# Latent heads: value products on half the columns, side by side, with the row sums made elsewhere

## The reference

```
def attend(q, k, v, scale):              # one head; context queries see the 256 context keys,
    s = q @ k.T * scale                  # latent queries all 768 keys
    p = exp(s - rowmax(s))
    return (p @ v) / rowsum(p)           # v is 64 wide
y  = attend(...) * silu(z)               # per head, then all heads beside each other
x  = x + gate * (concat(y_gla, y_latent, y_gqa) @ w_out)
```

## Time and profile before

| | |
|---|---|
| median of 3 runs | 957.71 us (954.34 to 958.46) |
| profiled execution, its own time | 957.99 us |
| its span in the trace | 956.2 us |
| TensorE busy | 911.3 us, 95% of the span |
| VectorE, ScalarE, GpSimd busy | 508.1, 432.6, 160.6 us |
| latent heads of layer 0 in the trace | 266.4 to 393.9 us |
| latent heads of layer 1 in the trace | 730.9 to 830.6 us |

### The profile page before, as it was taken

How to read it: one execution, slowest core, us unless ns; L and a number is a source line. 1 busy time by engine, 2 the same in 40 slices (tenths; PEclk the granted TensorE clock), 3 DMA queues, 4 the chain that set the end, 5 groups by cost and what they waited for, 6 DMA issues and landing times.

```text
span 956.2 us, 12848 instructions
## 1 busy us (share of the span) xinstructions
PE 911.3 (95%) x4607; PEld 665.2 (70%) x4607; DVE 508.1 (53%) x893; ACT 432.6 (45%) x809; POOL 160.6 (17%) x193
## 2 busy tenths in 40 slices
PE   4799999999999999899999999999999999899995
PEld 3488889888666666555588887889775656445584
DVE  4455424533547676756534655553646767455524
ACT  5434434321334545666831745543324445556712
POOL 1020000001442223002162000000026311002150
PEclk9899999999999999999999999999999999999998
DMA  9740230320202222222027102321401000222022
GB/s 342 276 125 22 50 83 22 89 66 2 88 1 88 89 88 88 89 91 86 1 77 215 65 22 67 92 64 42 113 23 67 1 1 1 89 88 89 1 110 89
DMA packets 67869, 74.21 MB, mean 78 GB/s; under 512 B 6148, under 2 KB 47456, under 8 KB 67680
## 3 DMA queue, kind: packets, MB, share of 16 engines
q1 hardware_dynamic: 61392, 60.24, 19.9%
q0 software_dynamic: 4016, 12.77, 3.8%
q10 hardware_dynamic: 2400, 0.38, 0.2%
HBM read 69.18 MB, written 4.19 MB: 77 GB/s over the span
## 4 chain that ended last, share of the span: by engine, by line
PE 85%; DVE 6%; ACT 4%; issue 3%; POOL 1%; ACTq 1%; DVEq 0%; POOLq 0%
PE pv L1868 12%; PE bank L1640 10%; PE bank L1641 9%; PE bank L1642 9%; PE bank L1954 4%; PE bank L1956 4%; PE bank L1955 4%; PE bank L1829 4%; PE bank L1795 2%; PE bank L1921 2%; PE bank L1915 2%; PE bank L1687 2%; PE bank L1686 2%; PE bank L1688 2%; PE bank L1591 2%
## 5 line engine op out<-in xcount | busy, mean ns | idle before, releaser
L1640 PE MATMUL bank<-hA_parts,W_parts 128*128 128x512 f32 (+1 forms) x480 | 174.6, 364 | 5.1 <-DVE h_low_parts L1155 5.1
L1641 PE MATMUL bank<-hA_parts,W_parts 128*128 128x512 f32 (+1 forms) x496 | 174.5, 352 | 0.0
L1004 ACT ACTIVATE hA<-bank 128x512 f32<-128x512 f32 (+1 forms) x168 | 93.3, 562 | 89.6 <-PE bank L1917 65.3
L1454 DVE TENSOR_REDUCE mxp<-bank 128x1 f32<-128x384 f32 x192 | 96.0, 551 | 33.7 <-PE bank L1829 33.2
L1640 PEld LDWEIGHTS bank<-hA_parts,W_parts 128*128 128x128 f32 x480 | 92.4, 192 | 22.4 <-issue 10.8
L1642 PE MATMUL bank<-h_low_parts,W_parts 128*128 128x512 f32 (+1 forms) x300 | 106.0, 353 | 0.0
L1641 PEld LDWEIGHTS bank<-hA_parts,W_parts 128*128 128x128 f32 x496 | 95.4, 192 | 13.2 <-issue 1.9
L1868 PE MATMUL pv<-hA,vg 128*128 128x512 f32 (+1 forms) x168 | 81.8, 571 | 4.4 <-ACT hA L1004 4.3
L1163 DVE TENSOR_TENSOR W_parts<-W,W_parts 128x1024 fp32r<-128x1024 f32 x43 | 52.5, 1222 | 36.7 <-ACT W_parts L711 36.7
L1868 PE MATMUL pv<-hA,h_low 128*128 128x512 f32 (+1 forms) x144 | 69.3, 562 | 0.0
L711 ACT ACTIVATE W_parts<-W 128x1024 fp32r<-128x1024 f32 x43 | 45.3, 1057 | 41.2 <-DMA W<-in_w_in 40.7
(11 more groups left out here) (291 smaller groups left out, 1914.3 us busy)
## 6 DMA issues: line engine op xcount, KB each, us to landing
W<-in_w_in SPq DMA_DIRECT2D x39, 512.0 KB, 4.1
W<-in_w_mod SPq DMA_DIRECT2D x8, 2048.0 KB, 8.1
W<-in_w_out SPq DMA_DIRECT2D x4, 2048.0 KB, 8.0
gqk<-in_w_mod SPq DMA_DIRECT2D x2, 1536.0 KB, 9.9
cqkv<-in_w_mod SPq DMA_DIRECT2D x2, 1536.0 KB, 14.2
XA<-in_x SPq DMA_DIRECT2D x4, 512.0 KB, 7.4
XA<-in_x POOLq DMA_DIRECT2D x4, 512.0 KB, 6.8
x_between_layers<-XA POOLq DMA_DIRECT2D x4, 512.0 KB, 3.0
```

The lines of the kernel that those rows point to most:

```text
L1004: act.activation(prob[slot % 4][:, 0:nq], ps("sc", l, h, q0, kt)[:, 0:nq], ACT.Exp, scale=MLA_SCALE if h < MLA_H else GQA_SCALE)\
L1454: dve.tensor_reduce(mxp[:, t, half:half + 1], ps("mx", l, h, q0, t, half)[:, 0:384], AX, ALU.max).then_inc(*up("part_max", l, h, q0, t, half))
L1640: pe.matmul(p[:, 0:c[1]], high[:, k, :], h_hi[:, k, toks], start=(k == 0), stop=False)
L1641: pe.matmul(p[:, 0:c[1]], low[:, k, :], h_hi[:, k, toks], start=False, stop=False)
```

## The change

For the latent heads alone:

- `vm` holds the values alone, [128, 6, 64] for each key tile. `pv` makes two products for each unit, one for each half of the queries, with the same 64 columns of values as weights; they write partitions 0 to 63 and 64 to 127 of one bank. Context and latent queries of a head share a bank now.
- The products are held back: `flush(2, most)` does nothing until 6 units are pending (layer 0) or 5 (layer 1), then it multiplies all but two; the rest follows ahead of `max_rows` of the next head. So a head has two runs of value products.
- The row sums: GpSimd adds probability buffers in pairs (`add_pair`: one of 256 columns for the context, two of 512, and one more add of the two), VectorE adds the last pair (`last_pair`), and TensorE multiplies the results by ones (`den`, three pairs of half-width products in layer 0, two in layer 1), after `project_k` of the next head.
- `recip` becomes one Ln and one Exp on all 128 partitions for both kinds of queries (`latent_recip`). `normalise` becomes two half-width products and the gate (`latent_normalise`), and that of the context queries moves from inside `maxima` to the start of the next head, ahead of that of the latent queries.
- GpSimd's `k_pad` and `q_pad(0)` move into head 5, behind that head's first `add_pair` in layer 0 and behind the sums of head 4 in layer 1. The ones in `vm` are no longer written.
- Six buffers `prob` in place of four.

```diff
+PROBS = 6
...
-        vm = [e.rearrange("p (r c) -> p r c", r=3) for e in
-              [low[:, T + 576 * t:T + 576 * t + 576] for t in range(TILES - 1)] +
-              [tz[:].rearrange("p a b -> p (a b)")[:, 0:576]]]
+        vm = [low[:, T + 384 * t:T + 384 * t + 384].rearrange("p (h v) -> p h v", h=MLA_H) for t in range(TILES)]
+        pair_sum = {0: [low[:, 4 * T + 512:5 * T]], 256: [low[:, 4 * T:4 * T + 512], XA[:, 7 * T - 256:7 * T + 256]]}
+        prob += [tz[:, i, :] for i in range(2)]
...
+        def half_cols(q0, nq):
+            c = 0 if q0 else 256
+            return slice(c, c + nq // 2)
...
-                for h in heads[1:MLA_H]:
-                    if h < len(out_tiles(l)):
-                        gla_in(out_tiles(l)[h])
-                        pool.wait_ge(*at("Sbd", l, out_tiles(l)[h], 1))
-                        two_diagonals(out_tiles(l)[h])
-                        pool.wait_ge(*at("A_both", l, out_tiles(l)[h]))
-                pool.wait_ge(*at("filled", "qp", l, MLA_H - 1, LAT))
-                for g in range(2):
-                    if g:
-                        pool.wait_ge(*at("k_pad", l, 0, 1))
-                    pool.memset(k_low[g][64:96, :].bitcast(F32), 0.0).then_inc(*up("k_pad", l, g, 0))
-                    pool.memset(k_low[g][96:97, :].bitcast(F32), 1.0).then_inc(*up("k_pad", l, g, 1))
-                pool.wait_ge(*at("k_pad", l, 1, 1))
-                for b in range(2):
+                def add_pair(h, q0, nq, i):
+                    slot, to = slot_of(l, h, q0) + 2 * i, min(i, 1)
+                    pool.wait_ge(*at("prob", l, slot + 1))
+                    if h:
+                        pool.wait_ge(*at("filled", "den", l, h - 1))
+                    if i:
+                        pool.wait_ge(*at("kd_exp", l, 1))
+                    pool.tensor_tensor(pair_sum[q0][to], prob[slot % PROBS][:, 0:nq],
+                                       prob[(slot + 1) % PROBS][:, 0:nq], ALU.add).then_inc(*up("pair_sum", l, h, q0, i))
+                def query_pad(b):
                     pool.wait_ge(*at("filled", "sc", l, MLA_H + b - 2, 256, TILES - 1))
                     pool.memset(q_high[b][64:96, :].bitcast(F32), 0.0).then_inc(*up("q_pad", l, b))
-                pool.wait_ge(*at("q_pad", l, 1))
+                    pool.wait_ge(*at("q_pad", l, b))
+                for h in heads[:MLA_H]:
+                    tile = out_tiles(l)[h + 1] if h + 1 < len(out_tiles(l)) else None
+                    if tile is not None:
+                        gla_in(tile)
+                    if len(qbs(l)) == 2:
+                        add_pair(h, *qbs(l)[0][:2], 0)
+                    if tile is not None:
+                        pool.wait_ge(*at("Sbd", l, tile, 1))
+                        two_diagonals(tile)
+                        pool.wait_ge(*at("A_both", l, tile))
+                    if h == MLA_H - 1:
+                        pool.wait_ge(*at("filled", "qp", l, MLA_H - 1, LAT))
+                        pool.wait_ge(*(at("pair_sum", l, h, 0, 0) if len(qbs(l)) == 2 else at("both_sums", l, h - 1)))
+                        for g in range(2):
+                            pool.memset(k_low[g][64:96, :].bitcast(F32), 0.0).then_inc(*up("k_pad", l, g, 0))
+                            pool.wait_ge(*at("k_pad", l, g, 0))
+                            pool.memset(k_low[g][96:97, :].bitcast(F32), 1.0).then_inc(*up("k_pad", l, g, 1))
+                            pool.wait_ge(*at("k_pad", l, g, 1))
+                        query_pad(0)
+                    for i in range(2):
+                        add_pair(h, *qbs(l)[-1][:2], i)
+                    pool.wait_ge(*at("pair_sum", l, h, 256, 1))
+                    pool.tensor_tensor(pair_sum[256][0], pair_sum[256][0], pair_sum[256][1], ALU.add)\
+                        .then_inc(*up("both_sums", l, h))
+                pool.wait_ge(*at("both_sums", l, MLA_H - 1))
+                query_pad(1)
...
+                def latent_recip(h):
+                    n = sum(nq // 2 for _, nq, _ in qbs(l))
+                    act.wait_ge(*at("filled", "den", l, h))
+                    if recips:
+                        act.wait_ge(*at("o_scaled", *recips[-1]))
+                    act.activation(rd[:, 0:n], ps("den", l, h)[:, 0:n], ACT.Ln).then_inc(*up("den_ln", l, h))
+                    let_go(("den", l, h), "den_ln", l, h)
+                    act.wait_ge(*at("den_ln", l, h))
+                    act.activation(rd[:, 0:n], rd[:, 0:n], ACT.Exp, scale=-1.0).then_inc(*up("recip", l, h))
+                    recips.append((l, h, 256))
...
+                def latent_normalise(h, q0, nq):
+                    cols, r, n2 = half_cols(q0, nq), 64 * (h % 2), nq // 2
+                    dve.wait_ge(*at("pv_filled", l, h, 256))
+                    if last_y[0]:
+                        dve.wait_ge(*at("y_attn", *last_y[0]))
+                    dve.wait_ge(*at("recip", l, h))
+                    for e in range(2):
+                        half = slice(64 * e, 64 * e + 64)
+                        dve.scalar_tensor_tensor(out=un[r:r + 64, n2 * e:n2 * e + n2], in0=pv_banks[h % 2][half, cols],
+                                                 scalar=0.5, in1=rd[half, cols], op0=ALU.mult, op1=ALU.mult)\
+                            .then_inc(*up("o_scaled", l, h, q0))
+                    dve.wait_ge(*at("o_scaled", l, h, q0))
+                    y = Y[r:r + 64, 2 + h // 2, q0:q0 + nq]
+                    dve.tensor_tensor(y, un[r:r + 64, 0:nq], y, ALU.mult).then_inc(*up("y_attn", l, h, q0))
+                    last_y[0] = (l, h, q0)
+                def last_pair(h):
+                    slot = slot_of(l, h, 256) + 4
+                    dve.wait_ge(*at("both_sums", l, h))
+                    dve.wait_ge(*at("prob", l, slot + 1))
+                    dve.tensor_tensor(pair_sum[256][1], prob[slot % PROBS], prob[(slot + 1) % PROBS], ALU.add)\
+                        .then_inc(*up("last_sum", l, h))
...
-                        normalise(h - 1, *qbs(l)[-1][:2])
+                        for q0, nq, nk in qbs(l) if h - 1 < MLA_H else qbs(l)[-1:]:
+                            normalise(h - 1, q0, nq)
...
+                    if h < MLA_H:
+                        last_pair(h)
...
+                        o, n2 = pv_banks[h % 2][:, half_cols(q0, nq)], nq // 2
+                        for e in range(2):
+                            mm = pe.matmul(o[64 * e:64 * e + 64], vm[kt][:, h, :], prob[sl % PROBS][:, n2 * e:n2 * e + n2],
+                                           start=(kt == 0), stop=(kt == nkt - 1), skip_group_check=True)
                     else:
-                        v = vg[:, kt, (h - MLA_H) // 3, 64 * e:64 * e + P]
-                    if h == 0 and kt == 0:
-                        pe.wait_ge(*at("vm", l, TILES - 1, 1))
-                        pe.wait_ge(*at("vg", l, TILES - 1, 1))
-                    mm = pe.matmul(pv_banks[i % 2][:, 0:nq], v, prob[sl % 4][:, 0:nq], start=(kt == 0),
-                                   stop=(kt == nkt - 1))
-                    if kt == nkt - 1:
+                        v = vg[:, kt, (h - MLA_H) // 3, 64 * (h % 2):64 * (h % 2) + P]
...
+                def den(h):
+                    p = open_("den", l, h)
+                    for q0, nq, nk in qbs(l):
+                        cols, n2 = half_cols(q0, nq), nq // 2
+                        parts = [(pair_sum[q0][0], ("both_sums", l, h)), (pair_sum[q0][1], ("last_sum", l, h))]\
+                            if q0 else [(pair_sum[q0][0], ("pair_sum", l, h, q0, 0))]
+                        for i, (part, ready) in enumerate(parts):
+                            pe.wait_ge(*at(*ready))
+                            for e in range(2):
+                                mm = pe.matmul(p[64 * e:64 * e + 64, cols], ones[:, 0:64], part[:, n2 * e:n2 * e + n2],
+                                               start=(i == 0), stop=(i == len(parts) - 1), skip_group_check=True)
+                    close(mm, "den", l, h)
+                def flush(keep_n, most=1):
+                    if len(pend) >= most:
+                        while len(pend) > keep_n:
+                            pv(*pend.pop(0))
...
-                    flush(1)
+                    flush(1 if h - 1 >= MLA_H else 0)
                     max_rows(h)
                     if h + 1 < len(heads):
                         project_k(h + 1)
                     flush(0)
+                    if 0 < h <= MLA_H:
+                        den(h - 1)
...
-                        flush(2)
+                        flush(2, 1 if h >= MLA_H else 6 if l < DEPTH - 1 else 5)
```

70 lines of the change are left out of this document (41 added, 29 removed).

## The result

The changed kernel takes 975.27 us in the median of 4 runs (974.97 to 979.69), the kernel before 956.77 us in four runs beside them. The ratio is 1.0196, with a 95% interval of 1.0179 to 1.0213: 1.9% slower, where I had forecast 960.9 us and a range up to 969. The profiled execution took 979.69 us, 4.4 us above the median; its mean granted clock was 0.973, that of the other three 0.977 to 0.978. What the two traces differ by, 21.6 us of span, is therefore 3.1 us more than what the medians differ by.

What follows compares the result with a forecast made beforehand. TensorE was taken to bound the kernel, with VectorE's masks just behind. Layer 0 +1.7, layer 1 -0.2 and clock +1.7 made +3.2 on 957.99, 961.2, or 960.9 us against the median; range 946 to 969.

Steps and rivals of the forecast that it cites:

- What bounds the kernel: Latent heads: TensorE, busy 95%, sets the time; VectorE's masks come only 1.2 us ahead of need.
- Value products: Latent heads: half-width products run in pairs, 0.27 us per run; TensorE alone is spared 12.1 us.
- VectorE, heads 1 to 4: Layer 0: masks 1.15 us later, a new 1.2 us wait; heads 1 to 3 gain about 0.0, head 4 -0.2.
- Head 5 and head 6 of layer 0: Head 5 waits for GpSimd's late memsets and `q_pad`, +0.9 us; head 6 starts behind VectorE's normalisations, +1.3 us.
- Layer 1: Heads 1 and 2 lose 0.65 us each, maskless heads 3 and 4 gain 0.9 each; sum -0.2 us.
- Clock: Head 5 of layer 0: the longer wait brings a stretch at the 1.2 GHz level, +1.7 us.
- C: Mask heads: VectorE operations stretch beside GpSimd, +4.2 us, and the clock drops once more, +1.7; 967 us, chance 0.25.
- B: Latent heads: the masks' cover is larger, so TensorE's saving of 12.1 us arrives; 945.9 us, chance 0.16.

Runs made afterwards that it cites:

- fill: Changed kernel with its first run of value products one unit earlier, right ahead of the waits for masks; 959.92 us, ratio 1.0022 to the kernel before.
- hold_wide: Kernel before, with full-width value products held back until five units are pending in layer 1's latent heads; 967.65 us, ratio 1.0105.
- late_ctx: Changed kernel with the context normalisation of the previous head moved behind the masks of the current one; 975.72 us, ratio 1.0168 to the kernel before.
- after_red1: Changed kernel with one more VectorE reduction, result unused, ahead of the masks of heads 1 to 4 of layer 0; 982.08 us, ratio 1.0251.
- delay6: Kernel before with six more VectorE reductions, results unused, ahead of the masks of heads 1 to 4 of layer 0; 968.27 us, ratio 1.0100.
- the two fillers: Changed kernel with extra products of constants, wide or narrow, ahead of the scores of the unit that waits for masks; 969.31 us and 970.38 us.
- spread: Changed kernel without the holding back, value products made once more than two units are pending; 975.26 us, ratio 1.0182 to the kernel before.
- five: Changed kernel with heads 0-4 context normalisation behind masks, earlier memsets, earlier first value run, and layer 1's low parts ahead of head 5's normalisation; 955.14 us, ratio 0.9973.

## Why the prediction was wrong, step by step

- **What bounds the kernel**: right. VectorE's masks were just behind TensorE, and the change put TensorE up against them in every masked head.
- **Value products**: right. They run in pairs; a run of four latent units at the end of head 1 took 311.93 to 313.81, 1.88 us, that is 1.73 and 0.15 for its edge, and `den` took 1.24 us. `fill` shows the saving, 0.95 us in head 1 where I had 1.1.
- **VectorE, heads 1 to 4**: right in kind. The masks ended 1.24 us later in heads 1 and 3, measured from `max_rows` (14.97 us for 13.73), and 1.56 in heads 2 and 4, where I had 1.15. TensorE waited 0.79 to 1.10 us, in two waits, where I had one of 1.2. I missed the second, 0.39 us, by which the second bank's masks come after the first bank's. Without the clock heads 1 to 4 lost 1.6 us, where I had -0.2.
- **Head 5 and head 6 of layer 0**: right in kind. The wait behind `q_pad` was 4.18 us (I had 3.8), and head 6 +1.4 (+1.3). Head 5 without its clock was +1.4 for +0.9. The products behind `q_pad` started 2.9 us later in the head than before, where I had 1.8 to 1.9 (and my own terms end at 386.14 us, which is 1.7): the second probabilities were ready 5.5 us into the head for 4.9, and from the first memset to the products it was 4.5 us for 3.9. For the add I also took "up to 1.3" beside VectorE, where the earlier trace rows has 1.65.
- **Layer 1**: heads 1 and 2 +0.9 and +0.7 beside the clock (I had +0.65 each). Head 3 was wrong: I gave it -0.9, since it has no masks, and it waited 1.25 us for the gate of the linear attention (L1407), the next thing of VectorE that was late; +0.6. Head 4 gave 0.5 of its 0.9. Sum +1.8 for -0.2.

```profile
814.31 0.41 PE L1916 MATMUL bank<-W_parts 96*128 96x384 f32 x1 [1.25 <-DVE YA L1407]
```

- **Clock**: this step failed. The prediction has one more stretch, "+1.7 us", behind the wait of head 5. There were seven more in the profiled execution, of 3.4 or 6.8 us, six of them in latent heads: the term was 14.4 us in the heads (16.1 with the stretch in the projections, which is not tied to the change) and some 12 in the medians, for 1.7. The forecast priced the new waits for the masks at their own length and gave them no clock, with no reason written down; the one row near it, the wait of 1.01 us in head 5 of layer 0 before, had cost none. That wait stood among full value products. The change had taken these out of the first half of a head, and behind the waits there a stretch stood in 5 of 8 heads, at 1.7 to 3.3 us each. The waits and the work were under-priced too, +6.2 us for +1.5, most of it in the bullets above. Of the 14.4 us between forecast and median some 10 are clock.

The rivals: C, the slower one, named both a longer VectorE and "the clock once more", and was nearest, with 967 us. That was partly luck: its price was 0.7 us of stretch in each masked head beyond the forecast, and the masks came only 0.1 to 0.4 us later than that in layer 0 and in heads 1 and 2 of layer 1; and it too was short of five stretches. B was not wrong that TensorE is spared something: `fill` comes 3.9 us under the kernel before, when half of the time for which TensorE is busy at half clock is taken off both spans (958.2 - 11.8 = 946.4 against 956.2 - 5.9 = 950.3), but that is a third of B's 12.1.

What is shown: the holding back makes the waits (`fill`, `hold_wide`), in layer 0 together with the later masks (`late_ctx`); the clock falls behind them often in the changed kernel (`after_red1`) and hardly in the kernel before (`delay6`); and behind work of either width in their place there was no stretch (the two fillers). What is open: how much the half width adds, which property of the work around a wait decides, and why the same code has a stretch in one execution and not in the next. What GpSimd's adds cost VectorE was read from rows alone and not tried apart.

## What to carry to other kernels

Work that is put off leaves its old place empty: before grouping an engine's cheap instructions, look at what that place was covering, and put the group where the engine would otherwise wait. One line that moved the run by one unit was worth 15 of the 18 us that the change lost. And price a new wait of TensorE at its length and the clock behind it, above all in a part of the kernel where the engine has just been given less to do; the granted clock of each stretch is the first thing to compare when TensorE is busy for longer with less work.

## What the runs showed of the hardware

- Half-width products, 64 weight columns each on its half of the partitions, overlap fully: eight pairs of passes of 256 columns take 1.73 us, 0.216 each, and a run costs 0.15 us at its end and about 0.09 us at its start.
- Waits of 1.58 to 1.85 us a head left the clock at 1.00 in four heads of `delay6`; waits of 1.36 to 1.71 us were followed by a clock of 0.50 in four heads of `after_red1`, for 3.4 us in three of them and 6.8 us in the fourth.
- Once down, the clock stayed down for 17.1 us in `spread`, where short runs of half-width products stand among the scores, and for 6.8 us with the same products in long runs (10.2 us once, in `five`).
- A gate of VectorE with 64x256 elements took 1.20 us beside GpSimd in head 1, where GpSimd made two elementwise products. The one of the earlier trace rows took 0.42 us beside GpSimd's memset of the earlier trace rows, no longer than with GpSimd idle. The mean over its six was 0.86 us, that of the twelve gates of this form before 0.47.
